# Around the turn from the products in pairs to attention: tables, rotary rows, key copies and gate weights loaded in another order, from other queues and in fewer transfers

## The chip, the cores and the metric

The kernel runs on one core of one Trainium2 chip. Its time is the device time of one launch in microseconds. Of three launches of the kernel before, the median is 1112.57 us (1110.75 to 1113.08).

## The reference

One decoder layer over 1024 tokens of width 1024, in float32. What matters here, cut short:

```python
h = rmsnorm(x, ln_pre)
z = h @ w_in      # c_val, c_glu, c_gate, q, k, v, a_gate, g_conv, g_attn
ya = conformer_conv(c_val, c_glu, ...) ; ya = (ya * silu(c_gate)) @ w_br_conv
yb = sliding_window_sink_attention(q, k, v, sinks, positions)
yb = (yb * silu(a_gate)) @ w_br_attn
m = sigmoid(g_conv) * ya + sigmoid(g_attn) * yb
x = x + rmsnorm(m @ w_out, ln_post)
x = x + sigmoid(x @ w_ple_gate) * (p @ w_ple_proj)
```

Attention has 16 query heads of 64 and 2 key and value heads, blocks and a window of 128. Of each head the first 16 of its 64 features are rotated (`partial_rope`, eight pairs, angles from `positions`); the other 48 pass through. So both queries and keys need tables of cosines and sines before the first score can be made.

## The kernel before, in words

Everything is kept transposed: features on the 128 partitions, the 1024 tokens along a row of 4 KB. A projection's output tile is 128 features by 1024 tokens. Each float32 product is three passes (high by high, low by high, high by low), so each weight tile is loaded raw, rounded by ScalarE (`w_hi`, `high`), and its rest is taken by VectorE or GpSimd (`w_lo`, `tile_low`, `low`) before TensorE may use it.

The stage before the turn ("early" products) makes most columns of `w_in` in pairs, seven products a pair (`early_product`). Its last pair is keys and values: keys end in `k_raw`, row 0 of `ring`, values in `v_t`, row 1. The query tiles 0, 1, 2, 4, 5, 6 were made there too and spilled to DRAM (`gates`, rows `3 * KT + j`); query tiles 3 and 7 (`PLAIN_Q`) are made next, as tiles `Q0` and `Q0 + 1`, in the ordinary way (L766, called by `tile`). While they run, the values are turned by TensorE (`turn_values`, L972) and copied by ScalarE (L1527 to L1530).

Then comes attention in 16 steps (`attention(p)`): step p makes the scores of a block of tokens and a key head (`scores`, L1015), half a tile of the attention gate (`a_gate`, tiles `C0` = 6 to 13; L1101), turns the probabilities of step p - 1 (L1033) and multiplies those of step p - 2 with the values (L1067, L1072). VectorE takes the maxima (L2209 to L2225) and normalises (L2232 to L2239), ScalarE makes the exponentials (L1558), all in an order written out by hand.

What must be there before the first score: `scores` waits for `conv_done`, for `k_dup` (both copies of both key heads in `kdup`: 4 transfers of the 48 plain features, 4 of the 16 rotated ones), for `unpacked[0]` (rotated query rows put back into `qo`) and for `last_roped` (tile 3 rotated where it lies).

Rotation: the rotary rows are gathered in `packs[0]` (two key heads, then tiles 0, 1, 2: 128 rows) and `packs[1]` (tiles 4, 5, 6: 96 rows), rotated by `rope(0)` and `rope(1)` on VectorE (L2167 to L2172, four instructions each), and sent back (`unpack`). Tile 3 is rotated in place by `rope_in_place(0, ...)` (L2183 to L2189, five instructions), after `rope(1)`; tile 7 later, in five pieces.

The order of SyncE's queue at the turn is written by hand: `load_tile(Q0)`, the second weight tile into `w_second`, a wait until all early products but the last are made (the places of `sin_t` and the packs are those of `early_hi`, their input), then `cos_t`, `sin_t` (L670), six transfers of 16 rotary rows (`pack`, L644), two of key rows (L675), six more, four plain key copies (L680), six whole query tiles of 512 KB (L683), the gate weights `load_tile(C0)`, `mixed` (L686), `unpack(0)` (which waits for `rope_done` and for all six query tiles), four rotated key copies (L690), `unpack(1)`, and `load_tile(C0 + 1)` (L592). ScalarE takes its instructions in order too: value copies, `query_tile(0)` (L1522), `high` of tile `C0` (L1356), `query_tile(1)`, then `high` of tile `C0 + 1` ahead of the exponentials of step 0.

The tables come out of `trig` in DRAM with a source that repeats the same rows: `cos_t` is 16 copies of 8 rows, `sin_t` 8 copies of 16 rows.

Of the kernel before, what the change touches and what calls it, by code (L numbers as in the profile page):

```python
# [17 lines left out]
F32 = mybir.dt.float32  # L18
# [7 lines left out]
P = 128  # L26
D = 1024
S = 1024
KT = D // P
# [23 lines left out]
C0 = 6  # L53
# [55 lines left out]
def build(nc, dram):  # L109
    with ExitStack() as ctx:  # L110
# [29 lines left out]
        cos_t = at("cos_t", [S], F32, RE + 12 * KB)  # L140
# [18 lines left out]
        v_last = at("v_last", [P], F32, GB + 28 * KB - 192)  # L159
# [250 lines left out]
        def pack_of(j):  # L410

            return (0, j + 1) if j < 3 else (1, j - 4)

# [174 lines left out]
        def _(sp):  # L588
# [51 lines left out]
            def pack(j):  # L640

                n, c = pack_of(j)
                for par in range(2):
                    sp.dma_start(packs[n][32 * c + 16 * par:32 * c + 16 * par + ROT, :],  # L644
                                 GATES[par * HD:par * HD + ROT, 3 * KT + j, :]).then_inc(packed[n], 16)

            def unpack(n):

                sp.wait_ge(rope_done, n + 1)
                sp.wait_ge(q_loaded, 96)  # L650
                for j in range(4 * n, 4 * n + 3):
                    c = pack_of(j)[1]
                    for par in range(2):
                        sp.dma_start(qo[par * HD:par * HD + ROT, j, :],
                                     packs[n][32 * c + 16 * par:32 * c + 16 * par + ROT, :]).then_inc(unpacked[n], 16)
# [4 lines left out]
            sp.dma_start(w_second[:], WALL[:, Q0 + 1 + PLE_STEPS, :]).then_inc(w_loaded[1], 16)  # L660
            sp.wait_ge(spilled[0], 16 * len(SPILLS))
            sp.wait_ge(spilled[1], 16 * len(SPILLS))
            sp.wait_ge(pos_loaded, TRIG_STORED)
            sp.wait_ge(early_made, EARLY_PRODUCTS - 1)
            def rows_of_angles(first, last):
                return TRIG[first:last].rearrange("n (f c) a -> (n f) (c a)", f=8).rearrange("(a r) s -> a r s", a=1)

            for table, first, last in ((cos_t, 0, 1), (sin_t, 1, 3)):
                count = 8 * (last - first)
                sp.dma_start(table[:], rows_of_angles(first, last).to_broadcast([P // count, count, S])).then_inc(pos_loaded, 16)  # L670
            for j in (0, 1, 2):
                pack(j)
# [3 lines left out]
            for j in (4, 5, 6):  # L676
                pack(j)
            for g in range(2):
                for half in range(2):
                    sp.dma_start(kdup[half * HD + ROT:(half + 1) * HD, g, :],  # L680
                                 k_raw[g * HD + ROT:(g + 1) * HD, :]).then_inc(k_dup, 16)
            for j in (0, 1, 2, 4, 5, 6):
                sp.dma_start(qo[:, j, :], GATES[:, 3 * KT + j, :]).then_inc(q_loaded, 16)  # L683
            load_tile(C0)
            sp.wait_ge(conv_done, KT)
            sp.dma_start(mixed[:], CONST[:, 1, :]).then_inc(masks_loaded, 16)  # L686
            unpack(0)
            for g in range(2):
                for half in range(2):
                    sp.dma_start(kdup[half * HD:half * HD + ROT, g, :], packs[0][ROT * g:ROT * g + ROT, :]).then_inc(k_dup, 16)  # L690
            unpack(1)
            load_tile(C0 + 1)
# [62 lines left out]
        def _(pe):  # L755
# [225 lines left out]
            def scores(p, jp):  # L981
# [365 lines left out]
        def _(act):  # L1347
# [175 lines left out]

            act.wait_ge(v_turned, 1)
# [5 lines left out]
            nc.scalar.activation(v_last[lower_half], turned_values[lower_half, NB - 1, :], ACT.Copy).then_inc(v_ready, 1)  # L1530
            query_tile(0)
# [340 lines left out]
        def _(dve):  # L1872
# [319 lines left out]
            rope(0, P, slice(0, S), 128)  # L2192
# [534 lines left out]
```

## Time and profile before

| | us |
|---|---|
| median of 3 launches | 1112.57 |
| the profiled launch | 1111.12 |
| its span, first to last instruction | 1109.3 |
| TensorE busy in the span | 1090.7 (98%) |
| VectorE, ScalarE, GpSimd busy | 884.9, 485.2, 316.2 |
| mean granted TensorE clock | 0.995 |

The profiled launch is 1.8 us longer than its span: that lies around the first and last instruction and is taken as fixed. All times in rows are us from the start of the span unless marked ns. "<-" in a wait names what ended it. An engine name with a q (SPq, ACTq) is its queue of issued transfers.

### The profile page before, as it was taken

The page shows a single profiled execution, that of the slowest core. Times are in us where ns is not written, and L with a number is a line of the kernel's source. Part 1 is how long each engine was busy: PE and PEld are TensorE (multiplying, and loading weights), DVE is VectorE, ACT ScalarE, POOL GpSimd, SP SyncE. Part 2 cuts the span into 40 slices and gives each one's busy share as a digit, 9 for nine tenths or more (in the row PEclk, how much of TensorE's full clock was granted, in tenths as well). Part 3 has the DMA queues.
Part 4 walks back from the last instruction along what each step waited for, and adds up shares of the span by engine and source line. Part 5 has one row for each costly group of instructions (what it writes and reads, how often), then busy time and mean ns, then how long its engine had stood idle before and what let it go on. Part 6 is the DMA issues. An engine that isn't in the chain of part 4 may idle for free.

```text
span 1109.3 us, 16255 instructions
## 1 busy us (share of the span) xinstructions
PE 1090.7 (98%) x5992; PEld 887.9 (80%) x5992; DVE 884.9 (80%) x1243; ACT 485.2 (44%) x927; POOL 316.2 (29%) x252
## 2 busy tenths in 40 slices
PE   9999999999999998799999999999999999999998
PEld 7888888888888886577777888888888888888887
DVE  5998989999999975598985788777768878466875
ACT  6633343443334432466674442433435426344332
POOL 1068888887888851200000000000000000000000
PEclk9999999999999999899999999999999999999999
DMA  9802231322232329777742111464544843344655
GB/s 343 350 1 78 78 113 42 114 77 77 94 134 77 114 80 236 206 208 198 187 131 77 39 57 38 133 217 143 180 134 129 319 137 127 95 128 138 192 188 189
DMA packets 52976, 155.19 MB, mean 140 GB/s; under 512 B 6281, under 2 KB 7049, under 8 KB 50857
## 3 DMA queue, kind: packets, MB, share of 16 engines
q1 hardware_dynamic: 38216, 96.58, 27.1%
q10 hardware_dynamic: 12384, 40.90, 10.5%
q0 software_dynamic: 2304, 16.78, 6.4%
q8 instruction: 43, 0.70, 0.2%
q14 instruction: 29, 0.23, 0.1%
HBM read 123.86 MB, written 45.19 MB: 152 GB/s over the span
## 4 chain that ended last, share of the span: by engine, by line
PE 91%; DMA 3%; SPq 2%; DVE 2%; ACT 1%; issue 1%; DVEq 0%; ACTq 0%
PE psg L766 31%; PE psg L953 31%; PE psb L1193 11%; PE psg L1101 7%; PE psg L790 2%; PE psg L1072 1%; PE psb L1015 1%; PE psg L1193 1%; DMA qo<-gates 1%; PE psg L873 1%; PE psg L819 1%; PE psg L1146 1%; PE psg L1033 1%; ACT probs L1558 1%; PE psg L1067 1%; DMA p_raw<-pT 1%
## 5 line engine op out<-in xcount | busy, mean ns | idle before, releaser
L1251 POOL TENSOR_TENSOR pair_w<-early_raw,pair_w 128x512 fp32r<-128x512 f32 x117 | 155.5, 1338 | 83.1 <-ACT pair_w L1443 83.1
L953 PE MATMUL psg<-early_hi,pair_w 128*128 128x512 f32 x576 | 177.3, 389 | 0.0
L2095 DVE SCALAR_TENSOR_TENSOR psb<-conv,cols,psb 128x510 f32<-128x510 f32 (+6 forms) x196 | 137.7, 745 | 0.0
L953 PE MATMUL psg<-h_hi,pair_w 128*128 128x512 f32 x432 | 133.0, 389 | 0.0
L953 PEld LDWEIGHTS psg<-early_hi,pair_w 128*128 128x128 f32 x576 | 108.1, 188 | 22.4
L1443 ACT ACTIVATE pair_w<-early_raw 128x512 fp32r<-128x512 f32 x117 | 71.4, 627 | 112.3 <-POOL early_raw L1267 81.1
L1234 POOL TENSOR_TENSOR rstd<-mean_sq,expo 128x4 f32<-128x4 f32 x3 | 3.1, 1020 | 382.9 <-DVE mean_sq L1896 363.4
L953 PE MATMUL psg<-early_lo,pair_w 128*128 128x512 f32 x288 | 112.0, 389 | 0.0
L1882 DVE TENSOR_TENSOR w_lo<-w_raw,w_hi 128x1024 fp32r<-128x1024 f32 x57 | 69.8, 1224 | 41.2 <-ACT w_hi L1356 37.5
L953 PEld LDWEIGHTS psg<-h_hi,pair_w 128*128 128x128 f32 x432 | 81.1, 188 | 16.8
L1356 ACT ACTIVATE w_hi<-w_raw 128x1024 fp32r<-128x1024 f32 x58 | 61.2, 1056 | 65.0 <-PE psg L766 34.6
L2095 DVE SCALAR_TENSOR_TENSOR psb<-fir_sum,fir_taps,psb 128x511 f32<-128x511 f32 (+14 forms) x120 | 89.4, 745 | 0.0
L953 PE MATMUL psg<-h_lo,pair_w 128*128 128x512 f32 x216 | 84.0, 389 | 0.0
L1267 POOL TENSOR_TENSOR early_raw<-early_raw 128x512 f32<-128x512 f32 x54 | 75.0, 1390 | 4.2
L1193 PE MATMUL psb<-s_hi,pair_w 128*128 128x512 f32 x240 | 73.9, 389 | 0.0
L953 PEld LDWEIGHTS psg<-early_lo,pair_w 128*128 128x128 f32 x288 | 54.1, 188 | 11.3
L766 PE MATMUL psg<-h_hi,w_hi 128*128 128x512 f32 x192 | 59.6, 392 | 0.0
L766 PE MATMUL psg<-h_hi,w_lo 128*128 128x512 f32 x192 | 59.2, 389 | 0.0
L766 PE MATMUL psg<-h_lo,w_hi 128*128 128x512 f32 x192 | 59.1, 389 | 0.0
L1675 ACT ACTIVATE pair_w<-block_raw 128x512 fp32r<-128x512 f32 x56 | 34.5, 626 | 41.7 <-PE psb L1193 21.5
L1193 PEld LDWEIGHTS psb<-s_hi,pair_w 128*128 128x128 f32 x240 | 45.0, 188 | 9.4
L1101 PE MATMUL psg<-h_hi,w_hi 128*128 128x512 f32 x128 | 52.1, 407 | 0.0
(348 smaller groups left out, 2511.8 us busy)
## 6 DMA issues: line engine op xcount, KB each, us to landing
w_raw<-weights SPq DMA_DIRECT2D x60, 512.0 KB, 3.6
gates<-ring ACTq DMA_DIRECT2D x30, 512.0 KB, 3.6
w_sums<-w_pairs POOLq DMA_DIRECT2D x12, 1024.0 KB, 8.5
ring<-gates ACTq DMA_DIRECT2D x24, 512.0 KB, 4.4
early_raw<-w_pairs SPq DMA_DIRECT2D x9, 1024.0 KB, 5.5
block_raw<-w_sums SPq DMA_DIRECT2D x32, 256.0 KB, 3.0
early_raw<-w_pairs SPq DMA_DIRECT2D x9, 768.0 KB, 4.6
block_raw<-w_pairs SPq DMA_DIRECT2D x24, 256.0 KB, 3.7
```

The source lines that it names most:

```text
L766: mm = nc.tensor.matmul(psg[:, slot, h * HALF:(h + 1) * HALF], w[:, wslot, (wk + k) * P:(wk + k + 1) * P], r[:, k, h * HALF:(h + 1) * HALF ...
L790: mm = nc.tensor.matmul(psg[:, slot, h * HALF:(h + 1) * HALF], w[:, slot, k * P:(k + 1) * P], r[:, k, h * HALF:(h + 1) * HALF], start=(k = ...
L953: mm = nc.tensor.matmul(bank, pair_w[:, at_w, w, k * P:(k + 1) * P], r[:, k, :], start=(not onto and k == 0 and m == 0), stop=(k == KP - 1 ...
L1101: mm = nc.tensor.matmul(gate_bank(p), w[:, t % 2, k * P:(k + 1) * P], r[:, k, half], start=(k == 0 and m == 0), stop=(k == KT - 1 and m == 2))
L1193: mm = nc.tensor.matmul(bank, pair_w[:, at_w, w, k * P:(k + 1) * P], r[:, k, :], start=(not onto and k == 0 and m == 0), stop=(k == KP - 1 ...
L1251: nc.gpsimd.tensor_tensor(pair_w[:, at_w, 1, :], early_source(s, n), pair_w[:, at_w, 0, :].bitcast(F32), ALU.subtract).then_inc(early_spli ...
L1267: nc.gpsimd.tensor_tensor(early_block(s, out), early_block(s, a), early_block(s, b), ALU.add).then_inc(early_summed, 1)
L1356: nc.scalar.activation(w_hi[:, j % 2, :], w_raw[:, j % 2, :], ACT.Copy).then_inc(w_hi_ready, 1)
L1443: nc.scalar.activation(pair_w[:, early_slot(b), 0, :], early_source(s, n), ACT.Copy).then_inc(early_split_hi, 1)
L1675: nc.scalar.activation(pair_w[:, pair_slot(b), 0, :], block_raw[:, b % 7, :], ACT.Copy).then_inc(pair_hi, 1)
L1882: nc.vector.tensor_tensor(w_lo[:, slot, :], w_raw[:, slot, :], w_hi[:, slot, :].bitcast(F32), ALU.subtract).then_inc(w_lo_ready, 1)
L2095: own.step(stt(acc[:, shift:], source[:, 0:HALF - shift], weight, acc[:, shift:], ALU.mult, ALU.add))
```

## The change

- `cos_t` moves to a place in the weight buffer of the early pairs that is free earlier, and is loaded before the wait for the spills and the early products; `sin_t` stays after it. `v_last` moves out of its way.
- The rotary rows come in 3 transfers of 32 rows for each pack (`rotary_rows`), in place of 6 of 16 rows; those of both packs are issued ahead of the key rows. The source of one is `GATES` seen as [2 halves, 16 rows, 1024], the destination 32 partitions.
- Of the six query tiles only the 48 plain rows of each half are loaded, 3 tiles in one transfer (`plain_rows`, 4 transfers of 576 KB), so `unpack` doesn't wait for them any more; `scores` does.
- `load_tile(C0)` goes ahead of the query rows, `load_tile(C0 + 1)` behind them and ahead of `unpack(0)`.
- The key copies (4 plain ones, 4 rotated ones) are issued by ScalarE: the plain ones before it waits for the turned values, the rotated ones after the value copies, behind a wait for `rope_done`, ahead of `query_tile(0)`.

```diff
-        cos_t = at("cos_t", [S], F32, RE + 12 * KB)
+        cos_t = at("cos_t", [S], F32, GB + 28 * KB - 192)
-        v_last = at("v_last", [P], F32, GB + 28 * KB - 192)
+        v_last = at("v_last", [P], F32, GB + 36 * KB - 192)
-            def pack(j):
-
-                n, c = pack_of(j)
-                for par in range(2):
-                    sp.dma_start(packs[n][32 * c + 16 * par:32 * c + 16 * par + ROT, :],
-                                 GATES[par * HD:par * HD + ROT, 3 * KT + j, :]).then_inc(packed[n], 16)
+            def rotary_rows(n):
+
+                for j in range(3):
+                    rows = GATES.rearrange("(par h) j s -> j par h s", par=2)[3 * KT + 4 * n + j, :, 0:ROT, :]
+                    first = 32 * (1 - n) + 32 * j
+                    sp.dma_start(packs[n][first:first + 32, :], rows).then_inc(packed[n], 16)
+
+            def plain_rows(n, par):
+
+                rows = slice(par * HD + ROT, par * HD + HD)
+                sp.dma_start(qo[rows, 4 * n:4 * n + 3, :], GATES[rows, 3 * KT + 4 * n:3 * KT + 4 * n + 3, :]).then_inc(q_loaded, 16)
             def unpack(n):
                 sp.wait_ge(rope_done, n + 1)
-                sp.wait_ge(q_loaded, 96)
...
+            def load_table(table, first, last):
+
+                count = 8 * (last - first)
+                rows = TRIG[first:last].rearrange("n (f c) a -> (n f) (c a)", f=8).rearrange("(a r) s -> a r s", a=1)
+                sp.dma_start(table[:], rows.to_broadcast([P // count, count, S])).then_inc(pos_loaded, 16)
             sp.wait_ge(early_made, EARLY_LAST)
             load_tile(Q0)
             sp.wait_ge(early_split_lo, EARLY_LAST)
             sp.dma_start(w_second[:], WALL[:, Q0 + 1 + PLE_STEPS, :]).then_inc(w_loaded[1], 16)
+            sp.wait_ge(pos_loaded, TRIG_STORED)
+            load_table(cos_t, 0, 1)
             sp.wait_ge(spilled[0], 16 * len(SPILLS))
             sp.wait_ge(spilled[1], 16 * len(SPILLS))
-            sp.wait_ge(pos_loaded, TRIG_STORED)
             sp.wait_ge(early_made, EARLY_PRODUCTS - 1)
-            for table, first, last in ((cos_t, 0, 1), (sin_t, 1, 3)):
-                count = 8 * (last - first)
-                sp.dma_start(table[:], rows_of_angles(first, last).to_broadcast([P // count, count, S])).then_inc(pos_loaded, 16)
-            for j in (0, 1, 2):
-                pack(j)
+            load_table(sin_t, 1, 3)
+            rotary_rows(0)
+            rotary_rows(1)
             main_read(sp, len(EARLY) - 1)
             for g in range(2):
                 sp.dma_start(packs[0][ROT * g:ROT * g + ROT, :], k_raw[g * HD:g * HD + ROT, :]).then_inc(packed[0], 16)
-            for j in (4, 5, 6):
-                pack(j)
-            for g in range(2):
-                for half in range(2):
-                    sp.dma_start(kdup[half * HD + ROT:(half + 1) * HD, g, :],
-                                 k_raw[g * HD + ROT:(g + 1) * HD, :]).then_inc(k_dup, 16)
-            for j in (0, 1, 2, 4, 5, 6):
-                sp.dma_start(qo[:, j, :], GATES[:, 3 * KT + j, :]).then_inc(q_loaded, 16)
             load_tile(C0)
+            for n in range(2):
+                for par in range(2):
+                    plain_rows(n, par)
+            load_tile(C0 + 1)
             sp.wait_ge(conv_done, KT)
             sp.dma_start(mixed[:], CONST[:, 1, :]).then_inc(masks_loaded, 16)
             unpack(0)
-            for g in range(2):
-                for half in range(2):
-                    sp.dma_start(kdup[half * HD:half * HD + ROT, g, :], packs[0][ROT * g:ROT * g + ROT, :]).then_inc(k_dup, 16)
             unpack(1)
-            load_tile(C0 + 1)
@@ scores, p = 0
                     pe.wait_ge(k_dup, 128)
+                    pe.wait_ge(q_loaded, 64)
                     pe.wait_ge(unpacked[0], 96)
@@ ScalarE
+            act.wait_ge(early_tanh, READ_BASE[len(EARLY) - 1] + READS[len(EARLY) - 1])
+            for g in range(2):
+                for half in range(2):
+                    act.dma_start(kdup[half * HD + ROT:(half + 1) * HD, g, :],
+                                  k_raw[g * HD + ROT:(g + 1) * HD, :]).then_inc(k_dup, 16)
             act.wait_ge(v_turned, 1)
...
             nc.scalar.activation(v_last[lower_half], turned_values[lower_half, NB - 1, :], ACT.Copy).then_inc(v_ready, 1)
+            act.wait_ge(rope_done, 1)
+            for g in range(2):
+                for half in range(2):
+                    act.dma_start(kdup[half * HD:half * HD + ROT, g, :], packs[0][ROT * g:ROT * g + ROT, :]).then_inc(k_dup, 16)
             query_tile(0)
@@ VectorE
-            rope(0, P, slice(0, S), 128)
-            rope(1, 96, slice(0, S), 96)
+            rope(0, P, slice(0, S), 80)
+            rope(1, 96, slice(0, S), 48)
```

## Rows read from the trace of the kernel before

**Rows 1.** The page, 40 slices of 27.7 us: tenths of busy time.

```profile
PE   9999999999999998799999999999999999999998
```

**Rows 2.** Windows: us; busy (x) of PE, PEld, DVE, ACT, POOL; clock, DMA, GB/s.

```profile
439.30:449.27 9.97, 0.00 (x1) 0.03 (x1) 5.22 (x5) 1.97 (x2) 4.07 (x2) 0.66 0.69 151
449.27:452.70 3.43, 3.43 (x19) 2.95 (x20) 2.02 (x4) 0.00 (x0) 0.00 (x0) 0.50 0.95 348
463.30:480.65 17.35, 16.45 (x232) 11.77 (x232) 15.52 (x35) 11.83 (x44) 1.89 (x3) 1.00 0.68 186
480.65:596.00 115.35, 115.35 (x1466) 84.91 (x1466) 101.79 (x205) 77.70 (x291) 7.61 (x11) 1.00 0.63 166
```

**Rows 3.** Waits of TensorE, 440 to 620: who <- whom, us, times, longest.

```profile
PE psb L1015 <- DMA kdup<-pack: 10.0, 1, 10.0
PE psg L1033 <- DVE probs L2239: 2.3, 1, 2.3
```

**Rows 4.** Timeline of SyncE's queue: start, us, queue, line, transfer.

```profile
414.03 0.59 SPq L670 DMA_DIRECT2D cos_t<-trig  x1
414.67 0.70 SPq L670 DMA_DIRECT2D sin_t<-trig  x1
415.42 2.72 SPq L644 DMA_DIRECT2D pack<-gates  x6
418.18 1.25 SPq L675 DMA_DIRECT2D pack<-ring  x2
...
441.17 3.68 SPq L654 DMA_DIRECT2D qo<-pack  x6
444.90 2.48 SPq L690 DMA_DIRECT2D kdup<-pack  x4
...
451.22 17.57 SPq L592 DMA_DIRECT2D w_raw<-weights  x3
```

**Rows 5.** Waits of SyncE's queue, 380 to 480, the one on the query tiles.

```profile
SPq L650 <- DMA qo<-gates: 10.6, 1, 10.6
```

**Rows 6.** Timeline of VectorE: the rotations, the first sinks.

```profile
428.14 0.01 DVE L2167 LOAD_MASK_SELECT rtmp<-pack  x1 [13.49 <-DMA pack<-ring]
...
431.91 1.23 DVE L2172 TENSOR_TENSOR pack<-pack,rtmp 128x1024 f32<-128x1024 f32 x1
...
438.42 0.01 DVE L2183 LOAD_MASK_SELECT rtmp<-qo  x1
...
443.41 1.22 DVE L2189 TENSOR_TENSOR qo<-work,rtmp 16x1024 f32<-16x1024 f32 x1
...
453.78 0.17 DVE L2225 TENSOR_TENSOR esink<-sinks,smax 128x8 f32<-128x8 f32 x1
```

**Rows 7.** Timeline of ScalarE at the turn.

```profile
422.29 0.27 ACT L1530 ACTIVATE v_last<-psg 64x128 f32<-64x128 f32 x1
428.52 1.03 ACT L1522 ACTIVATE qo<-psg 128x1024 f32<-128x1024 f32 x1 [5.96 <-PE psg L766]
...
457.26 1.06 ACT L1356 ACTIVATE w_hi<-w_raw 128x1024 fp32r<-128x1024 f32 x1 [12.93 <-DMA w_raw<-weights]
458.22 0.39 ACT L1558 ACTIVATE probs<-probs,nmax 128x128 f32<-128x128 f32 x1
```

**Rows 8.** Transfers, 412.0 to 442.3: packets by size; issues, KB, us to landing.

```profile
DMA packets 2137, 6.51 MB, mean 215 GB/s; under 512 B 440, under 2 KB 568, under 8 KB 2136
...
pack<-ring SPq DMA_DIRECT2D x2, 64.0 KB, 9.1
qo<-pack SPq DMA_DIRECT2D x2, 64.0 KB, 2.3
```

**Rows 9.** Windows: us, clock, DMA share, GB/s, at first data and in the query tiles.

```profile
415.00:415.50 0.50, 1.00 0.49 66
433.50:439.50 6.00, 1.00 1.04 414
```

**Rows 10.** Timeline of GpSimd: the low part of the first gate tile.

```profile
443.50 3.32 POOL L1244 TENSOR_TENSOR w_lo<-w_raw,w_hi 128x1024 fp32r<-128x1024 f32 x1 [20.43 <-ACT w_hi L1356]
```

More of the change, by code:

```diff
@@ L408, in leave @@
                 self.base, self.n = self.before + self.per * times, 0
-        def pack_of(j):
-            return (0, j + 1) if j < 3 else (1, j - 4)
         def ple_slot(t):
@@ L638, in load_tile @@
                 load_weights(t + PLE_STEPS, t % 2, t + 1)
-            def pack(j):
-                n, c = pack_of(j)
-                for par in range(2):
-                    sp.dma_start(packs[n][32 * c + 16 * par:32 * c + 16 * par + ROT, :],
-                                 GATES[par * HD:par * HD + ROT, 3 * KT + j, :]).then_inc(packed[n], 16)
+            def rotary_rows(n):
[6 more added lines that the diff above has]
+                sp.dma_start(qo[rows, 4 * n:4 * n + 3, :], GATES[rows, 3 * KT + 4 * n:3 * KT + 4 * n + 3, :]).then_inc(q_loaded, 16)
             def unpack(n):
                 sp.wait_ge(rope_done, n + 1)
-                sp.wait_ge(q_loaded, 96)
-                for j in range(4 * n, 4 * n + 3):
-                    c = pack_of(j)[1]
+                for j in range(3):
                     for par in range(2):
-                        sp.dma_start(qo[par * HD:par * HD + ROT, j, :],
-                                     packs[n][32 * c + 16 * par:32 * c + 16 * par + ROT, :]).then_inc(unpacked[n], 16)
+                        first = 32 * (1 - n) + 32 * j + ROT * par
+                        sp.dma_start(qo[par * HD:par * HD + ROT, 4 * n + j, :], packs[n][first:first + ROT, :]).then_inc(unpacked[n], 16)
+            def load_table(table, first, last):
+                count = 8 * (last - first)
+                rows = TRIG[first:last].rearrange("n (f c) a -> (n f) (c a)", f=8).rearrange("(a r) s -> a r s", a=1)
+                sp.dma_start(table[:], rows.to_broadcast([P // count, count, S])).then_inc(pos_loaded, 16)
             sp.wait_ge(early_made, EARLY_LAST)
@@ L660, in _ @@
             sp.dma_start(w_second[:], WALL[:, Q0 + 1 + PLE_STEPS, :]).then_inc(w_loaded[1], 16)
+            sp.wait_ge(pos_loaded, TRIG_STORED)
+            load_table(cos_t, 0, 1)
             sp.wait_ge(spilled[0], 16 * len(SPILLS))
             sp.wait_ge(spilled[1], 16 * len(SPILLS))
-            sp.wait_ge(pos_loaded, TRIG_STORED)
             sp.wait_ge(early_made, EARLY_PRODUCTS - 1)
-            def rows_of_angles(first, last):
-                return TRIG[first:last].rearrange("n (f c) a -> (n f) (c a)", f=8).rearrange("(a r) s -> a r s", a=1)
-            for table, first, last in ((cos_t, 0, 1), (sin_t, 1, 3)):
-                count = 8 * (last - first)
-                sp.dma_start(table[:], rows_of_angles(first, last).to_broadcast([P // count, count, S])).then_inc(pos_loaded, 16)
-            for j in (0, 1, 2):
-                pack(j)
+            load_table(sin_t, 1, 3)
+            rotary_rows(0)
+            rotary_rows(1)
             main_read(sp, len(EARLY) - 1)
```

## The prediction

> **What bounds the kernel now.** I read the page by slices first, then windows, then the waits of TensorE, and from the wait that stands out back through the queues. TensorE is at 9 tenths in every slice but two neighbours [rows 1]. These two are the turn: no product in 9.97 us, from 439.30, where the second query tile ends, to 449.27; then 3.43 us with a granted clock of 0.50, the lower level (1.2 GHz), after which it is back at 1.00; and a second stall of 2.3 us [rows 2, 3]. From 480.65 on TensorE has no gap at all (115.35 of 115.35), so what is won or lost at the turn reaches the end whole [rows 2].
>
> The first stall ends with the key copies. Followed back: `kdup<-pack` goes out at 444.90, behind six `qo<-pack` from 441.17, and these stood 10.6 us behind the whole query tiles, though the rotation they also wait for was done at 433.1 [rows 4 to 6]. VectorE's own last step, `rope_in_place(0)`, ends at 444.63. So two chains run side by side: one ends at 449.27, the other at 444.6, 16.5 us after VectorE's first rotation begins at 428.14, which is when the last row of `packs[0]` lands [rows 6]. That start, X below, sets everything that follows.
>
> The second stall: after the scores the maxima and sinks are ready at 453.95, but the exponentials begin at 458.22, since ScalarE first takes `high` of tile `C0 + 1`, whose load was issued last, at 451.22 [rows 4, 6, 7].
>
> **What goes.** `unpack(0)` no longer waits for whole query tiles; it can go at rotation's end, X + 5.0, needs 3.7 us of issue and 2.3 to land: X + 11. The key copies by ScalarE go at the same time: 2.5 us of issue, landed by X + 10. `load_tile(C0 + 1)` is issued before either. So the first chain shrinks below VectorE's: the first score comes at X + 16.5 [rows 4, 6, 8]. The second stall goes with it: the exponentials could start 4.1 us sooner. TensorE keeps not all of that; it gets 2.3 us of the named wait [rows 3] and at most 0.9 more, for in 463.30 to 480.65 it lacks 0.90 us [rows 2]. I take 3.0.
>
> **What ScalarE's part costs.** Four issues at 0.62 us ahead of the value copies make these end 2.5 us later, 425.1 for 422.6; the second query tile, which needs them, starts at about 428 [rows 4, 7]. Behind the new wait for `rope_done` stand `query_tile(0)`, `high` of `C0`, `query_tile(1)`. They start at X + 5.0 + 2.5; the copy of the query tile is done at X + 8.5, `rope_in_place(0)` wants it at X + 10.3; `high` of `C0` ends at X + 9.6, its low part on GpSimd 3.3 us later, X + 13, all under VectorE's 16.5 [rows 6, 7, 10]. Nothing, then, but the cover is VectorE's chain, and 1.8 us is the thinnest place. GpSimd's sums of weights start as much later as the gate tile's low part; no gap of TensorE up to 596 shows anyone waiting for them [rows 2].
>
> **What decides: when X comes.** Queue order alone would bring it forward: `cos_t` moves to about 398.5, and the 12 transfers for packs become 6. But count engines. In 412.0 to 442.3, 28 transfers land (the two tables, 14 for packs, 4 key copies, 6 query tiles, one weight tile, `mixed`). A transfer leaves one tiny packet for each DMA engine it used; at 16 each that is 448, and there are 440 under 512 B [rows 8]. Eight are missing, as if one transfer had used 8 engines. The odd one is `sin_t`: its source is 8 copies of 16 rows, where `cos_t` has 16 copies, and its issue takes 0.70 us against 0.59 [rows 4]. I read: a transfer is spread over as many engines as its outermost source dimension has entries, up to 16. The new rotary source is [2, 16, 1024]: two engines, the same two for all six.
>
> (The Trainium skill, "DMA: Bandwidth & Descriptors", section "Why a DMA increments its semaphore by 16 and not by 1", says that the number of engines is the largest one up to 16 that divides the slowest dimension of both patterns, and that they are the lowest-numbered. The 440 agree with it; which engines they are no row shows.)
>
> Now the two engines' work ahead of X, in 4 KB packets. First data came 1.2 us after the first issue, 415.2 [rows 4, 9]; the issue stays at 414.03, behind the wait for the early products.
> - `sin_t`: 16 packets. Of such mixed work the eight loaded engines did 8 + 16 + 8 = 32 packets in 428.1 - 415.2 = 12.9 us, 0.40 each [rows 6]. In a full stream a packet takes 16 x 4096 B / 414 GB/s = 0.158 [rows 9]. Bounds 2.5 and 6.4; I take 6.4, since tables and small transfers are what that mix was.
> - Six rotary transfers: 6 x 16 = 96 packets of distinct rows, two engines alone in their part of SBUF, nearest to the stream: 96 x 0.158 = 15.2. Bounds: 0.158 and 0.40, so 15.2 to 38.4.
> - Four key copies from ScalarE's queue, 48 rows each: 12 packets in between, 1.9 (to 4.8; 0 if they slip into `sin_t`'s pauses).
> - Two key-row transfers at the very end: 2 packets, 0.8.
>
> X = 415.2 + 6.4 + 15.2 + 1.9 + 0.8 + 0.2 (wake) = 439.7, against 428.1. First score at 439.7 + 16.5 = 456.2: 6.9 us later than 449.27. Less 3.0: +3.9 us. Against the profiled launch 1111.12 + 3.9 = 1115.0; the median stood 1.45 above that launch, so 1116.5. The plain query rows come behind X on these engines: 8 + 4 x 9 packets of 0.158, X + 7, and `C0 + 1` at X + 8.3: covered. The idle of TensorE grows from 10 to 17 us; its clock falls and comes back as before.
>
> **Rivals.**
> - *All 16 engines carry the rotary rows* (the change does what its words say). Then they are 12 packets an engine, 1.9 to 4.8, take 3.6: X = 415.2 + 6.4 + 3.6 + 1.9 + 0.8 + 0.2 = 428.1. No gain for X, but the first chain is gone: first score 444.6, 4.7 us sooner, and 3.0: -7.7, so 1105 (1101 to 1108). For it: the SBUF side has 32 partitions, and 16-row transfers used 16 engines. Against it: the missing eight. Chance 0.13.
> - *Two engines, but tables and copies at stream speed*: `sin_t` 2.5, copies hidden: X = 433.9, first score 450.4, +1.1 - 3.2 = -2.1: 1110.5. Break-even is X = 435.8. Chance 0.22 for the region within 2.2 us of no change, at most.
> - *Two engines and slow packets*: at 0.20 to 0.40 the rotary rows take 19.2 to 38.4: +8 to +27, 1120 to 1140. For it: 16-row transfers were slow in the same places. Against: 16 engines pushed into the same 16 partitions there, here two. Chance 0.12.
> - The forecast itself, +2.2 to +8: 0.53.
>
> (The Trainium skill, same page, section "Rules for kernel authors", advises to coalesce many small transfers into large ones. By it alone fewer rotary transfers win, and the result would be the first rival's, about 1105. No row shows a coalesced transfer of this shape.)
>
> **How the numbers follow.** The predicted time is 1116.5. The low end, 1110.5, is the fast-copies case; the high end, 1123, takes key copies at 4.8 and rotary packets at 0.20 (+2.9 +4.0 on 1116.5, rounded). Left out are the first rival and the slowest packets, under 0.2 in all. A measurement of this kernel can tell about 0.2% (2.2 us) from no change. Faster: 0.13 and 0.02 from the second rival's tail, 0.15. Same: 0.22 and 0.03 of the forecast's lower edge, 0.25. Slower: the rest, 0.60.
>
> **What the profile after would show.** VectorE's first rotation at 438 to 442, ended by a pack's transfer, and the DMA share near 2/16 for some us before it: two engines. At 428 or before: the first rival. First score 16.5 us after the rotation starts, behind VectorE, not behind a transfer; if a transfer ends that wait, my covers are wrong. Exponentials of step 0 straight after the sinks, and no 2.3 us wait at the first turning. If first score minus rotation start is over 17, ScalarE's new wait has struck. From the second turning on, TensorE without a gap, as before [rows 2]. The forecast falls if the rotary transfers don't run on two engines.

## The result, and the profile of the kernel after

The changed kernel took 1127.18 us (1124.97 to 1127.66), beside 1112.82 for the kernel before (four launches of each): ratio 1.0127, 95% interval 1.0107 to 1.0147. The sign was forecast. The size was not: 1116.5, with a range that ended at 1123.

The profiled launch took 1127.06 us, its span is 1125.2. Page, TensorE in 40 slices of 28.1 us, to be held against [rows 1]:

```profile
PE   9999999999999996399999999999999999999998
```

The dip is the turn again, and deeper. Windows of the kernel after, columns as in [rows 2]:

```profile
440.15:467.71 27.56, 0.01 (x2) 0.04 (x1) 16.49 (x16) 3.84 (x4) 3.11 (x2) 0.54 0.62 135
467.71:471.10 3.39, 3.39 (x19) 2.94 (x20) 1.98 (x4) 0.00 (x0) 0.88 (x1) 0.50 0.93 237
...
472.10:473.10 1.00, 1.00 (x4) 0.81 (x3) 0.91 (x6) 0.68 (x3) 0.00 (x0) 0.50 0.99 205
...
499.00:614.00 115.00, 115.00 (x1471) 84.11 (x1471) 100.98 (x201) 78.08 (x291) 7.40 (x11) 1.00 0.61 162
```

No product for 27.56 us, where it was 9.97. Waits of TensorE, 430 to 640: one is left, and it ends with VectorE, not with a key copy; the 2.3 us of [rows 3] are gone.

```profile
PE psb L1009 <- DVE qo L2192: 27.6, 1, 27.6
```

VectorE, to be held against [rows 6]:

```profile
450.39 0.01 DVE L2170 LOAD_MASK_SELECT rtmp<-pack  x1 [34.90 <-DMA pack<-ring]
...
462.03 1.80 DVE L2188 TENSOR_TENSOR rtmp<-rtmp,sin_t 128x1024 f32<-128x1024 f32 x1
...
466.24 1.22 DVE L2192 TENSOR_TENSOR qo<-work,rtmp 16x1024 f32<-16x1024 f32 x1
...
472.21 0.17 DVE L2228 TENSOR_TENSOR esink<-sinks,smax 128x8 f32<-128x8 f32 x1
```

It stood 34.90 us for the last row of `packs[0]`; its first rotation began at 450.39 for 428.14, and the first score came at 467.71 for 449.27. SyncE's queue, to be held against [rows 4]:

```profile
414.88 0.70 SPq L660 DMA_DIRECT2D sin_t<-trig  x1
415.63 3.88 SPq L641 DMA_DIRECT2D pack<-gates  x6
419.56 7.66 SPq L676 DMA_DIRECT2D pack<-ring  x2
427.26 0.58 SPq L588 DMA_DIRECT2D w_raw<-weights  x1
427.88 2.41 SPq L646 DMA_DIRECT2D qo<-gates  x4
430.34 0.97 SPq L588 DMA_DIRECT2D w_raw<-weights  x1
...
455.39 8.84 SPq L654 DMA_DIRECT2D qo<-pack  x12
```

Everything for `packs[0]` was issued by 427.2, and it took until 450.2 to land. What the transfers did meanwhile (windows of the kernel after: clock, DMA share, GB/s; cut where, by the trace's completion records, one rotary transfer ends and the next goes on):

```profile
425.60:429.80 4.20, 1.00 0.54 132
429.80:435.00 5.20, 1.00 1.09 223
435.00:441.90 6.90, 1.00 1.00 158
441.90:447.20 5.30, 0.56 0.92 181
447.20:450.20 3.00, 0.50 0.15 52
```

The last line shows the two engines: a share of 0.15 is about 2 of 16, and 52 GB/s over two is 4096 B in 0.158 us each. The three lines above it show what was not forecast: all 16 engines at work, and one rotary transfer of 16 packets an engine taking 5.2 to 6.9 us, 0.33 to 0.43 a packet. The completion records also say that the two engines did nothing else of SyncE's queue in between: their shares of `C0` and of the plain rows land between 451.35 and 457.73, behind the last pack row, where the other fourteen were through with the same transfers by 446.3.

**The account.** The span grew by 15.9 us. Of that, 0.85 is there already where the second query tile ends (440.15 for 439.30). The first products start on time; 0.6 comes from a wait for ScalarE at 10 us, the rest before 100 us, and nothing in the change reaches there. It is scatter: in the traces of all runs below this tile ends between 438.6 and 440.2. So starts in two traces are compared to no better than some 1.5 us, or are counted from the issue of `sin_t`. The first score is 18.44 us later, 17.6 without the shift. Behind it, to the end of the span, 2.5 come back: 17.6 + 0.85 - 2.5 = 15.9.

### The profile page after: what moved, and what is told of

Read it like the earlier page. It is cut to its first block, busy times and chain, and to the rows that moved or that the text cites. A ratio compares the mean times of both kernels' runs of the same rounds, so it can differ in the third digit from the quotient of the medians.

```text
span 1125.2 us, 16245 instructions
## 1 busy us (share of the span) xinstructions
PE 1091.5 (97%) x5992; PEld 888.8 (79%) x5992; DVE 885.5 (79%) x1243; ACT 485.1 (43%) x927; POOL 316.1 (28%) x252
## 4 chain that ended last, share of the span: by engine, by line
PE 92%; DMA 3%; DVE 3%; SPq 1%; ACT 1%; issue 0%; DVEq 0%; ACTq 0%
PE psg L759 31%; PE psg L946 30%; PE psb L1187 10%; PE psg L1095 8%; DMA pack<-ring 2%; PE psg L783 2%; PE psb L1009 2%; PE psg L1066 1%; PE psg L1187 1%; PE psg L866 1%; PE psg L812 1%; PE psg L1140 1%; PE psg L1027 1%; PE psg L1061 1%; DMA p_raw<-pT 1%; PE psb L866 1%
## 5 line engine op out<-in xcount | busy, mean ns | idle before, releaser
L2394 DVE TENSOR_TENSOR pair_w<-block_raw,pair_w 128x512 fp32r<-128x512 f32 x56 | 37.9, 685 | 18.3 <-ACT pair_w L1678 18.3
```

What stands on the lines that cost most here:

```text
L2394: nc.vector.tensor_tensor(pair_w[:, at_w, 1, :], block_raw[:, b % 7, :], pair_w[:, at_w, 0, :].bitcast(F32), ALU.subtract).then_inc(pair_l ...
```

## The experiments

My theory after this result: the two engines cause the loss, through packets that are slow while the other fourteen run the gate weights and the query rows. Rivals: the loss lies in the plain query rows, in ScalarE's part, or in the order of the gate weights. Each run has the kernel before beside it (1111.5 to 1112.4 us), so across groups of runs the ratios are compared.

### All 16 engines again (e1_rows16)

In the kernel after, only the rotary transfers are undone (and the counts of their waits).

```diff
-                    sp.dma_start(packs[n][first:first + 32, :], rows).then_inc(packed[n], 16)
+                    for par in range(2):
+                        first = 32 * (1 - n) + 32 * j + ROT * par
+                        sp.dma_start(packs[n][first:first + ROT, :],
+                                     GATES[par * HD:par * HD + ROT, 3 * KT + 4 * n + j, :]).then_inc(packed[n], 16)
```

> The changed kernel with one part undone: the rotary rows come again in 12 transfers of 16 rows (source of 16 rows, so 16 engines) instead of 6 of 32; order, ScalarE's copies, gate weights and plain rows as changed. Theory A (in the changed kernel the six transfers run on two engines, and these hold back the first rotation until 450.4): the first rotation starts at about 427 to 430, the first score 16.5 us later, the time falls by about 20 us, to 1104 to 1109, below the kernel before. Theory B (not the engines but the new order, both packs ahead of the key rows and ScalarE's copies in between, holds them back): the rotation starts after 440 and the time stays above 1117.

1114.8 us, ratio 1.0028 (1.0018 to 1.0039). The rotation began at 431.44, 17.6 us from the issue of `sin_t` where it had been 35.5, so the two engines were the cause of 18 us there. The kernel before needs 13.5 (414.67 to 428.14): the start is still some 4 us late, of which more under the tenth run. Only 11 us of 14 came back (1.0127 - 1.0028), and 1104 to 1109 was wrong: TensorE now waited for something else. Waits of TensorE, then SyncE's queue, of this run:

```profile
PE psb L1010 <- DMA qo<-pack: 15.3, 1, 15.3
```

```profile
424.26 2.05 SPq L647 DMA_DIRECT2D qo<-gates  x4
...
436.49 8.86 SPq L655 DMA_DIRECT2D qo<-pack  x12
```

The sending back went out at rotation's end, as I had it, and took 12.9 us to land (median), where [rows 8] have 2.3. Windows of this run (clock, DMA share, GB/s): full engines, half the rate of [rows 9]. Beside the plain rows ScalarE's key copies are under way in both (from 436.49), GpSimd's sums in the second (from 443.81).

```profile
436.00:440.00 4.00, 1.00 1.05 218
...
444.00:448.00 4.00, 0.50 1.02 162
```

### The gate weights and plain rows held back (e2_hold_loads)

```diff
+            sp.wait_ge(packed[0], 80)
             load_tile(C0)
```

> The changed kernel with one wait more: SyncE waits until the first pack is complete before it issues the gate weights, the plain query rows and the second gate tile. The six rotary transfers stay as they are. Theory A1 (rotary packets are slowed because the other 14 engines stream those loads beside them): rotary packets take about 0.16 us each, the first rotation starts at about 440 to 442 instead of 450.4, the time falls by 8 to 10 us, to 1117 to 1119. Theory A2 (packets on the two engines are slow by themselves, whatever the others do): rotation start and time stay within 2 us of the changed kernel, 1125 to 1129.

1125.29 us, ratio 1.0126 (1.0109 to 1.0143). VectorE, then windows of this run:

```profile
439.82 0.01 DVE L2171 LOAD_MASK_SELECT rtmp<-pack  x1 [25.09 <-DMA pack<-ring]
```

```profile
434.00:439.80 5.80, 1.00 0.11 45
...
446.00:450.00 4.00, 0.50 0.95 154
450.00:454.00 4.00, 0.50 0.97 167
```

With none of these loads beside it the rotary chain ended at 439.82; the forecast was 439.7. By the completion records the first two rotary transfers took 3.9 us each, with ScalarE's key copies in between, and the other four 2.5 each, 0.156 a packet. So its working holds for two engines that are alone, and 9.8 us (25.7 from the issue of `sin_t` for 35.5) are what the streams beside it cost. What the two engines share with the other fourteen, and so why they slow down, no run here shows. Yet no time was won, where 8 to 10 us were expected: the four plain-row transfers, issued from 440.10, now ran at 154 to 167 GB/s, the last until about 459, the sending back behind them, and the first score came at 466.08, ended by `qo<-pack`. Two costs lie on top of each other.

### The plain rows in 4 KB packets (e3_plain_4k)

```diff
-                sp.dma_start(qo[rows, 4 * n:4 * n + 3, :], GATES[rows, 3 * KT + 4 * n:3 * KT + 4 * n + 3, :]).then_inc(q_loaded, 16)
+                for j in range(4 * n, 4 * n + 3):
+                    sp.dma_start(qo[rows, j, :], GATES[rows, 3 * KT + j, :]).then_inc(q_loaded, 16)
```

> The changed kernel with the plain query rows in 12 transfers of one tile (48 rows of 4 KB) instead of 4 of three tiles (48 rows of 12 KB). Same bytes, same engines. Theory A1a (the 12 KB packets, which took over 1 us each, are what crowds the two engines): the first rotation starts 5 us or more earlier, the time is 1117 to 1121. Theory A1b (any stream of the other engines crowds them alike, or the narrow destination of 48 partitions does): within 3 us of the changed kernel, 1124 to 1130.

(TensorE's wait counts 192 instead of 64.) 1124.97 us, ratio 1.0121 (1.0104 to 1.0138), rotation at 448.65, 35.2 us from the issue of `sin_t` for 35.5. Twelve transfers instead of four ran no faster: 173 GB/s at a share of 1.03 from 430.6 to 444.4. The length of their packets isn't what slows the rotary rows, nor themselves.

### The kernel before with the rotary transfers alone (e4_before_rot32)

```diff
-            for j in (0, 1, 2):
-                pack(j)
+            rotary_rows(0)
...
-            for j in (4, 5, 6):
-                pack(j)
+            rotary_rows(1)
```

> The kernel before with one part of the change alone: the rotary rows in 6 transfers of 32 rows (two engines) instead of 12 of 16; all else as before, the tables late, whole query tiles, key copies from SyncE. Theory A: rotation start 433 to 444 instead of 428, and the whole query tiles, which queue behind on the same two engines and hold the sending back, land after 450 instead of 441; slower than before by 10 us or more, 1122 to 1135. Theory B (fewer transfers are harmless or good by themselves): within 2 us of the kernel before or faster, 1110 to 1115.

1124.65 us, ratio 1.0119 (1.0102 to 1.0136): this one edit makes nearly the whole loss. VectorE and SyncE's queue of this run:

```profile
444.12 0.01 DVE L2172 LOAD_MASK_SELECT rtmp<-pack  x1 [6.71 <-DMA pack<-gates]
```

```profile
427.61 7.37 SPq L688 DMA_DIRECT2D qo<-gates  x6
...
453.35 3.69 SPq L661 DMA_DIRECT2D qo<-pack  x6
```

Here the first pack came early (432.37, three transfers ahead of the key rows), the second was waited for, and the whole query tiles had their last packets on the same two engines behind it: by the completion records fourteen engines were through with all six by 442.4, the last two between 446.3 and 453.28. `unpack(0)` went out at 453.35 for 441.17, and the first score came at 464.80.

### Whole query tiles, rotary rows on two engines (e5_whole_tiles_two)

```diff
                 sp.wait_ge(rope_done, n + 1)
+                sp.wait_ge(q_loaded, 96)
...
-            for n in range(2):
-                for par in range(2):
-                    plain_rows(n, par)
+            for j in (0, 1, 2, 4, 5, 6):
+                sp.dma_start(qo[:, j, :], GATES[:, 3 * KT + j, :]).then_inc(q_loaded, 16)
```

> The changed kernel with the plain query rows undone: six whole query tiles of 512 KB, 128 rows each, in their place, and the sending back waits for them as before. The rotary rows stay on two engines. Theory C (transfers into 48 rows are slow by themselves, 3.7 us for 576 KB against 1.3 us for 512 KB into 128 rows, and crowd the two engines while they last): the other engines are through by about 431, rotary packets are crowded for less long, the first rotation starts at 440 to 444 instead of 450.4, the first score comes about 17 us after it; 1115 to 1120. Theory D (any stream on the other engines crowds the two engines alike): rotation start 447 or later, 1122 to 1128.

1123.63 us, ratio 1.0104 (1.009 to 1.0119), rotation at 446.97, 32.3 us from the issue of `sin_t` for 35.5. Both kinds of stream slow the two engines. Beside whole tiles a rotary packet took 0.23 to 0.26 us, beside narrow ones up to 0.43, and X comes 3.2 us sooner. The wait for the first score ended with `qo<-pack`, sent at 456.62: the tiles' last packets stood behind the rotary ones on the two engines, and the last of them landed at 456.56.

### Both undone (e6_whole_tiles_rows16)

The edits of the first and of the fifth run together. Of the change there remain the early cosines, `C0` ahead of the query tiles, `C0 + 1` ahead of the sending back, and ScalarE's key copies.

> Both undone: rotary rows in 12 transfers of 16 rows and whole query tiles; of the change there remain the early cosines, gate weights ahead of query rows, the second gate tile ahead of the sending back, and ScalarE's key copies. Theory C: first rotation at about 431 as in the run with 16-row transfers, query tiles landed by about 441, first score at 448, behind VectorE and no longer behind a transfer; 1107 to 1110, faster than the kernel before, which is the gain of the early second gate tile and a little. Theory D or any other in which ScalarE's new wait or the order itself costs something: 1112 or more.

1109.62 us, ratio 0.9982 (0.9972 to 0.9991), rotation at 433.19. Waits of TensorE and a window (clock, DMA share, GB/s) of this run:

```profile
PE psb L1009 <- DVE qo L2192: 11.0, 1, 11.0
```

```profile
434.00:440.50 6.50, 1.00 1.03 409
```

The same rows as whole tiles: 409 GB/s, 1.28 us for 512 KB. Against the first run this is the price of the plain rows alone: 1.0028 - 0.9982, 5 us.

### The plain rows from another source (e7_plain_other_source)

The first run's kernel, with the 48-row transfers reading `xT`, whose rows lie 32 KB apart as its own tiles do; the queries are then other numbers.

```diff
-                sp.dma_start(qo[rows, 4 * n:4 * n + 3, :], GATES[rows, 3 * KT + 4 * n:3 * KT + 4 * n + 3, :]).then_inc(q_loaded, 16)
+                sp.dma_start(qo[rows, 4 * n:4 * n + 3, :], XT[rows, 4 * n:4 * n + 3, :]).then_inc(q_loaded, 16)
```

> The kernel with 16-row rotary transfers and plain rows, but the plain rows are read from the input x (rows 32 KB apart in DRAM) instead of the spilled gates (rows 128 KB apart), so the queries are other numbers. Theory C1 (the narrow destination of 48 rows makes these four transfers slow): they land as late as with the gates as source, about 3.5 us apart, first score at about 454, 1113 to 1117. Theory C2 (the far-apart source rows make them slow): about 1.4 us apart, first score at about 448, 1107 to 1111.

1115.36 us, ratio 1.0034 (1.0024 to 1.0044), 235 GB/s at a share of 0.97 from 438 to 442. Another source, with rows 32 KB apart instead of 128, brought no time back, though the rate is a little higher than the first run's 218; and the whole tiles of the sixth run are read from the same far-apart rows at 409. So the 48-partition destination is what remains. That it is the destination was inferred by exclusion, not varied by itself.

### Both tables ahead (e8_tables_early)

The sixth run's kernel, with `sin_t` in a place that is free earlier too, and the query tiles in two halves, so that each sending back waits for its own.

```diff
-        sin_t = at("sin_t", [S], F32, RE + 16 * KB)
+        sin_t = at("sin_t", [S], F32, GB + 32 * KB - 192)
...
-                sp.wait_ge(q_loaded, 96)
+                sp.wait_ge((q_loaded, q_late)[n], 48)
...
+            sp.wait_ge(early_split_lo, EARLY_LAST + PLACE[P7] + 1)
+            load_table(sin_t, 1, 3)
...
-            load_table(sin_t, 1, 3)
             rotary_rows(0)
-            rotary_rows(1)
```

(`rotary_rows(1)` follows the key rows; tiles 0 to 2, `C0`, tiles 4 to 6, `C0 + 1` behind it.)

> A version made from the findings: both tables loaded before the last early product (sin_t in the place of two more weight blocks), rotary rows in 16-row transfers, first pack and key rows ahead of the second pack, whole query tiles with a semaphore for each three, ScalarE's key copies, both gate tiles ahead of the sending back. If the engines' queues are what sets the start of the rotation: rotation starts at 421 to 424, first score at 439.5 to 441, almost without a stall; 1097 to 1102. If the start is set by something else (issue on SyncE, crowding by ScalarE's copies): rotation at 427 or later, 1104 or more.

1102.5 us, ratio 0.9912 (0.9896 to 0.9928): the fastest so far, 10 us under the kernel before and just above the range expected: the rotation began in time, the first score at 443.06, 2 us later than 441. The edits of this run (`sin_t` early, key rows ahead of the second pack, tiles in halves) weren't priced one by one. VectorE and the waits of TensorE:

```profile
421.91 0.01 DVE L2174 LOAD_MASK_SELECT rtmp<-pack  x1 [7.99 <-DMA pack<-ring]
```

```profile
PE psb L1013 <- DMA qo<-pack: 4.5, 1, 4.5
```

### `C0 + 1` early, alone (e9_before_c1_early), and with the sums held (e11_c1_early_sums_held)

In the kernel before:

```diff
             load_tile(C0)
+            load_tile(C0 + 1)
...
-            load_tile(C0 + 1)
```

> The kernel before with one edit: the weights of tile C0 + 1 are issued right after those of tile C0, ahead of the wait for the query tiles, in place of last. Theory A (the second stall, 2.3 us of named wait, and the slice of lacking time behind it are caused by ScalarE standing in front of C0 + 1, which is issued last): the exponentials of step 0 start right behind the sinks, at 454 to 455 in place of 458.2, the wait at the first turning is gone, the first score stays at 449.3 (to 450.6, if the 1.3 us of the transfer push the sending back), and the time is 2.3 to 3.2 us less: 1108.3 to 1109.2, with the push up to 1110.5. Theory B (the gain of the stall is given back at the next place, since ScalarE or VectorE then limit steps 0 and 1): the wait goes but the time stays within 1 us of the kernel before.

1112.13 us, ratio 0.9998 (0.9986 to 1.001): no change, and not for the reason theory B gave. The second stall was gone, but the first had grown. Waits of TensorE and GpSimd's timeline of the ninth run:

```profile
PE psb L1015 <- DMA kdup<-pack: 13.5, 1, 13.5
```

```profile
446.13 0.79 POOL L1337 DMA_DIRECT2D w_sums<-w_pairs  x1
```

GpSimd had finished the low part of `C0` 0.6 us sooner (2.35 us for the 3.32 of [rows 10]), and at the same place VectorE's last rotary instruction took 3.32 us for 1.22:

```profile
443.84 2.35 POOL L1244 TENSOR_TENSOR w_lo<-w_raw,w_hi 128x1024 fp32r<-128x1024 f32 x1 [20.45 <-ACT w_hi L1356]
443.95 3.32 DVE L2189 TENSOR_TENSOR qo<-work,rtmp 16x1024 f32<-16x1024 f32 x1
```

In the kernel before VectorE began first (443.41 for 443.50) and GpSimd had the long one; here GpSimd began first. So an order decided by 0.1 us sets when the sums go out. GpSimd sent 1 MB of weight sums on their way at 446.13, beside the last key copies (issued from 445.24), which now took a median of 3.8 us to land, for 2.4. The trace is of one launch of 1112.74 us; the eleven launches run from 1108.43 to 1115.22, the widest spread of all runs, and whether the others went the same way isn't known. The eleventh run adds one wait to GpSimd's program, ahead of the sums:

```diff
+            pool.wait_ge(k_dup, 128)
             for g in range(2):
```

> The kernel of e9_before_c1_early (before, with C0 + 1 issued right after C0) and one more edit: GpSimd waits for both copies of the keys (k_dup at 128) ahead of its first sum of weights. That sum's 1 MB went out at 446.13 there, while the rotated key copies were on their way (issued from 445.24), and the first score came 3.5 to 4 us later than before. Theory A (the sum's transfer got in front of the key copies): the copies land at about 449.5, the first score is at 449.3 to 450, the second stall stays away, and the time is 2 to 3.2 us less than the kernel before, ratio 0.997 to 0.998. Theory B (the copies were late for another reason, such as C0 + 1 itself): the first score stays at 452 to 453.5 and the ratio at 0.9998 or above.

1108.75 us, ratio 0.997 (0.996 to 0.9979), as theory A had it: the copies 2.3 us, no second stall. Waits of TensorE and GpSimd of this run:

```profile
PE psb L1015 <- DMA kdup<-pack: 10.1, 1, 10.1
```

```profile
449.54 0.79 POOL L1338 DMA_DIRECT2D w_sums<-w_pairs  x1 [2.62 <-DMA kdup<-pack]
```

So the second stall is worth 3.3 us, and it was a transfer from an engine off the critical path that took them.

### Key copies back on SyncE (e10_copies_on_sync)

The sixth run's kernel without ScalarE's part:

```diff
-            act.wait_ge(early_tanh, READ_BASE[len(EARLY) - 1] + READS[len(EARLY) - 1])
-            ... act.dma_start(kdup[half * HD + ROT:(half + 1) * HD, g, :], ...)
-            act.wait_ge(rope_done, 1)
-            ... act.dma_start(kdup[half * HD:half * HD + ROT, g, :], ...)
+            ... sp.dma_start(kdup[half * HD + ROT:(half + 1) * HD, g, :], ...)
             load_tile(C0)
...
             unpack(0)
+            ... sp.dma_start(kdup[half * HD:half * HD + ROT, g, :], ...)
             unpack(1)
```

> The kernel of e6_whole_tiles_rows16 (whole query tiles, 16-row rotary transfers on all engines, cosines early, both gate tiles early) with the eight key copies issued by SyncE again, four behind the key rows and four between the two sendings back, as in the kernel before. It prices the part of the change that gives them to ScalarE. Theory A (they cost nothing there, and gain little): rotation starts within 1 us of e6's 433.2, the rotated key copies are issued some 4 us after the sending back starts (446) and land at about 450, level with VectorE's end, so the first score is at 450 to 451.5 and the time is 1109 to 1111. Theory B (ScalarE's new wait and its issues cost something through the value copies, the second query tile or high of C0): with them back on SyncE the time is 1 to 2.5 us less than e6's, 1107 to 1108.5.

1113.6 us, ratio 1.0012 (1.0003 to 1.0021). Neither theory: without ScalarE's part the kernel is 3.3 us slower than the sixth run's. Waits of TensorE, and GpSimd:

```profile
PE psb L1016 <- DMA kdup<-pack: 15.6, 1, 15.6
```

```profile
437.98 0.79 POOL L1338 DMA_DIRECT2D w_sums<-w_pairs  x1
446.62 0.88 POOL L1340 DMA_DIRECT2D w_sums<-w_pairs  x1 [7.85 <-DMA w_sums<-w_pairs]
```

The copies go out at 446.04, behind `unpack(0)` and its wait for the query tiles, where ScalarE sent them at 438.25; that is right with the second of the sums, they take a median of 4.5 us to land, and TensorE waits for the last of them for 15.6 us, where it waited 11.0 for VectorE. ScalarE's wait for `rope_done` also had kept `high` of `C0`, and so the sums, back. The part was worth having, and for a reason I had not named.

It has a price too. VectorE's first rotation, sixth run and tenth:

```profile
433.19 0.01 DVE L2170 LOAD_MASK_SELECT rtmp<-pack  x1 [18.22 <-DMA pack<-ring]
```

```profile
430.19 0.01 DVE L2168 LOAD_MASK_SELECT rtmp<-pack  x1 [14.68 <-DMA pack<-ring]
```

From the issue of `sin_t` that is 18.9 and 15.3 us: with the plain key copies from SyncE behind the key rows, instead of from ScalarE beside the rotary rows, X comes 3.6 us sooner. The kernel before needs 13.5; for the 1.8 left the second pack ahead of the key rows is the likeliest reason, not tried alone. (The Trainium skill, "DMA: Bandwidth & Descriptors", section "Issuing engines are not separate DMA queues", says that a second issuing engine saves only the time to issue, usually a small thing. Here the second queue saved more, since it also passed by a wait that the copies didn't need: 7.8 us of start for 2.5 us of issue.)

### Both tables ahead, with the sums held (e12_tables_early_sums_held)

The eighth run's kernel with `pool.wait_ge(unpacked[0], 96)` ahead of the sums.

> The kernel of e8_tables_early with one edit: GpSimd waits until the rotated rows of tiles 0 to 2 are back (unpacked[0] at 96) ahead of its first sum of weights, whose 1 MB went out at 434.63 there, while that sending back (issued from 429.94) was landing until 442.9. Theory A (the sum delayed it): the last row is back by 440, the first score comes at 439.6 to 440.5 in place of 443.06, behind VectorE, and the time is 2.5 to 3.5 us less than e8's 1102.5: 1099 to 1100, ratio 0.988 to 0.989. Theory B (the query tiles ahead of it on the queue were the cause): the first score stays at 442 to 443 and the ratio at 0.991. Should the sums be needed sooner than I think, a wait of a block's weights would show behind 600 us.

1101.94 us, ratio 0.9905 (0.989 to 0.992), not to be told from 0.9912: theory B. The sums went out at 443.23 instead of 434.63, and TensorE still waited 3.7 us for `qo<-pack`. By the completion records the last query tile lands at 438.70, `C0 + 1` at 440.24, and the first rows sent back follow from 440.23 to 442.93. So what stands ahead on the queue is left as the likely cause; it wasn't tried.

## Why the prediction was right and wrong, step by step

- **Two engines carry the rotary rows: right**, and shown three times: by the last window (share 0.15, 52 GB/s), by the completion records, in which each of the six transfers ends with the reports of two engines, and by the first run, where the rotation begins 18 us sooner with 16 of them. The missing eight packets of [rows 8] were a true sign. (The rule in the Trainium skill, "DMA: Bandwidth & Descriptors", section "Why a DMA increments its semaphore by 16 and not by 1", gives two engines for a source that begins with a dimension of 2: the trace agrees.)
- **X = 439.7: wrong, 450.39 (449.5 without the shift). This is the step that failed**, and in it one term: six rotary transfers at 0.158 a packet, 15.2 us. With key copies and key rows that was 17.9; the completion records give 28.3, from 421.93, where `sin_t` had landed (5.9 us for 6.4), to 450.26. The key copies account for about 2.8 of it (1.9 forecast; from the second run's 3.9 and 2.5) and the key rows for 0.4 (0.8 forecast), so the rotary rows took some 25 for 15.2. I took the rate of a full stream and argued that two engines alone in their part of SBUF would keep it. The second run shows that they do if nothing runs beside them. What I left out is that the same change puts `C0`, the plain rows and `C0 + 1` on the queue right behind, and that fourteen idle engines begin on these at once. The forecast's own 0.40 a packet in mixed work had been the warning. It stood as the third rival, "two engines and slow packets", 1120 to 1140, at 0.12: that was the case, at the price it gave; its reason (narrow transfers are slow in those places) is not the one that the second run shows.
- **First score at X + 16.5: 17.3.** The forecast had set 17 as the sign that ScalarE's new wait has struck, and it did, for 0.6 us: one multiply took 1.80 us where its like took 1.22. GpSimd's low part of `C0`, which comes behind that wait, ran from 460.37 to 462.74 and lies over its start. The kept traces settle that this is the cause. In eleven of them a VectorE instruction that reads two tiles, like this one, begins while the low part runs, and each time it ends 1.08 or 1.09 us behind the low part's end, whether it took 1.80 us or 3.32. The other way round, where VectorE's instruction began first, the low part ends 2.2 to 2.3 us behind it (ten traces, this and the kernel before among them); where nothing is in its way it takes 2.3 to 2.4 us. So the 3.32 us of [rows 10] hold about 0.9 of waiting. The 0.25 us from VectorE's end to the first score (467.46 to 467.71) weren't in the sum. Nor would the multiply be free without ScalarE's wait: in the tenth run the low part comes sooner, falls on another multiply and costs 1.05. No transfer ended the wait in the kernel after: VectorE did, the rotated copies had gone out at 455.39 and the exponentials began at 472.42, right behind the sinks.
- **Fill gain 3.0: 2.5.** Gaps of 2.04 and 0.90 us (453.7 to 463.1, 463.30 to 480.65) went to 0.05 in the like stretches. But "its clock falls and comes back as before" was wrong: granted 0.50 (1.2 GHz) lasted until 473.2, 5.5 us from the first score, where it had been 3.4. The longer stall isn't shown to be the reason: in the other runs the lower level lasts 5.9 us of products after a stall of 4.5 (eighth), 5.5 after 10.1 (eleventh) and 4.2 after 15.6 (tenth). What it cost can be read: from the first score to the first turning it is 12.69 us for 14.05 (480.40 and 463.32 at the turning), 1.4 less although a wait of 2.25 us is gone, so about 0.9 went to the slower clock.
- **ScalarE's part at nothing: nearly right in the kernel after**, since VectorE came last; it took the 0.6 us above. In a kernel with the rotary rows mended it gains 3.3 us net, though it makes X 3.6 us later, which I hadn't put a sign to.
- **Plain rows covered at X + 7: right in the kernel after, wrong in its price.** The last of them landed at 457.73, X + 7.3. But I gave 36 packets of 0.158, and the first run shows 218 GB/s into 48 partitions (154 to 167 in the second, with more transfers beside them), the sixth 409 as whole tiles. They were hidden only because X was so late; with X mended they set the first score and cost 5 us. **The first rival's 1105 was wrong too**: 16 engines gave 1114.8. About half of that miss is the plain rows. The rest is mainly its X = 428.1, which came at 431.44 in the first run and at 433.19 in the sixth, with whole tiles and still 1109.6.
- **From 499 on no gap: right**, 115.00 of 115.00.

Taken alone, by ratios: the two-engine transfers cost 1.2% in the kernel before (13 us) and 1.0% in the kernel after (11); the plain rows 0.5% (0.2% in the kernel after, from the fifth run); ScalarE's copies gain 0.3%; `C0 + 1` early gains 0.3% if the sums are held and nothing otherwise. What is left without the two kinds of narrow transfer and without ScalarE's part (the tenth run: early cosines, both gate tiles early, all rotary rows ahead of the key rows) comes to +0.1%.

## What to carry to other kernels

A merged transfer can use fewer engines or fewer partitions than the ones it replaces, and here each of the two cost more than the merging gave: look at the outermost dimension of both sides first, and count its small packets in the trace after. Price a packet by what will run beside it once the queue has been rearranged, not by the row that is nearest in shape. And ask of each engine off the critical path what it sends when it is done sooner: here 1 MB of sums went out ahead of the last two of four small copies and took back the whole gain of another edit.

## What the runs showed of the hardware

- A transfer of 4 KB packets on two engines ran at 0.158 us a packet alone (52 GB/s for both), at 0.23 to 0.26 beside whole query tiles on the other fourteen (fifth run) and at 0.33 to 0.43 beside 48-row transfers.
- 48-row transfers ran at 173 to 247 GB/s with all engines busy, in 12 KB and in 4 KB packets and from two sources, and at 154 to 167 with more transfers beside them (second run); 128-row transfers of the same data at 409.
- An issue can stand: with the two engines' queue long, the two of `pack<-ring` took 7.66 us on SyncE in place of 1.25 [rows 4], and everything behind them on the queue went out that much later. In the third run twelve issues of plain rows took 13.84 us. That the long queue is the reason wasn't tested.
- VectorE's float32 instructions that read two tiles and GpSimd's low part, which reads two, don't run at the same time (the shuffle, which reads one, does: 460.64, 1.35 us, inside the low part). The one that begins second ends a fixed time behind the first, 1.08 us (VectorE, eleven traces) or 2.2 to 2.3 us (GpSimd, ten). Which one begins first also decides when the next 1 MB goes out: 443.41 before 443.50 gave 3.32 us on GpSimd, 443.95 behind 443.84 gave 3.32 us on VectorE.
